# Exchanging the rotary halves by a VectorE shuffle on reordered columns, with the cosines on GpSimd, in a two-layer fp32 transformer block

## The chip, the cores and the metric

The kernel runs on 1 core of one Trainium2 chip. The metric is the device time of one execution in microseconds; the time before is the median of 3 runs. All engine times below are microseconds from the start of the span of one profiled execution.

## The reference

Two layers (`DEPTH = 2`) over 256 tokens `x` and 256 context tokens, model width 1024. Each layer is: a feed-forward block, a mixer, a second feed-forward block, each behind an RMS norm whose shift, scale and gate come from a conditioning vector. The last layer computes no output for the context tokens. The mixer projects the normed tokens by `w_in`; the parts that matter here are the attention's queries and keys:

```python
q = axial_rope(rmsnorm(aq.reshape(B, S, 8, 128), q_norm_w), tabs)
k = axial_rope(rmsnorm(ak.reshape(B, S, 2, 128), k_norm_w), tabs)
kc = rmsnorm(akc.reshape(B, L, 2, 128), k_norm_w)          # context: not rotated

def rotate_pairs(x, cos, sin):            # x: 64 of a head's 128 features
    x1, x2 = jnp.split(x, 2, axis=-1)     # 32 and 32
    return jnp.concatenate([x1 * cos - x2 * sin, x1 * sin + x2 * cos], axis=-1)
```

`axial_rope` does this for the first 64 features with the angle of the token's row and for the last 64 with that of its column. So feature p is combined with feature p + 32 or p - 32. Scores are sums over the 128 features of a head, so any order of the features that q and k share gives the same scores. The rest of the mixer (window attention with a sink, a gated linear attention, two gated branches, an output projection) is not touched.

## The kernel before

One program, written engine by engine, with semaphores set by hand; the order of the work on each engine is the order of the code. Features lie on the 128 partitions and tokens on the free axis (512 in layer 0; in layer 1 the keys and values have 512 and the queries 256).

**Weights.** They stream as 1024 x 256 units, numbered through the program, into `raw` (two buffers by parity). For each unit ScalarE rounds `raw` to `WH` (`prep`, L707, its casts are L718) and VectorE computes the remainder `WL = raw - WH` (`prep`, L1178, its subtractions are L1184). TensorE then forms each product in three passes of matmuls (high x high, high x low, low x high). A unit has two halves e = 0, 1 of 128 columns, which is one output tile (m) each; `hi_ready` and `lo_ready` count the halves, and TensorE waits for the half that it needs. ScalarE's casts and VectorE's subtractions run two units at most ahead.

**The place of the change** is `attn_proj(l)`, the stretch in which the six units `n` to `n + 5` are used: the values (`n`), the keys (`n + 1`) and four units of queries (`n + 2` to `n + 5`, two heads each). The keys are tile pair j = 1, the queries j = 2 to 5. The first two units are used by `first_two`, while the norm's output `hH`, `hL` is still being made: token half c = 0 of unit `n` (L1952 to L1959), then c = 0 of unit `n + 1` (m = 0, then the norm's sums over the partitions for c = 1 at L2121, then m = 1; matmuls L1982, L1983, L1986), then both for c = 1. The norm code of ScalarE and VectorE casts unit `n + 1` between pieces of the norm:

```python
                if n:
                    prep(second, only=0)
                    for kt in range(WAIT_C[n] + 1, KT):
                        square(n, kt, 1)
                    prep(second, only=1)
                    log(1)
```

VectorE has `residual(n, kt, 1)` at the place of `square`, and each square waits for its residual.

Behind that, unit by unit (`unit_cols`, matmuls L1901, L1902, L1907): ScalarE copies a pair's tiles out of PSUM with the norm's weight (`weighted`, L869, into `qrs` for even j and `qn` for odd j), takes squares (`squares`, L851), and rounds the rotated tile (`split`, L883). VectorE normalizes the keys (`k_normed`, L1488), sums squares (`square_sums`, L1504), and computes the remainder (`low`, L1522). The rotation itself takes: `swaps(j)` on TensorE (L2288, two products of a 128 x 128 permutation `swap` with the two tiles, 256 tokens, back into the pair's own PSUM banks), `cosines(j)` (L1499) into `qt[:, e, 0]`, `sines(j)` (L1510) from PSUM into `qt[:, e, 1]` and `rotated(j)` (L1515) on VectorE. Only the 256 `x` tokens are rotated. After the queries come `gate_cols(l, 0, 0)` (L1921 to L1926), its copy out of PSUM on ScalarE (L915, which lets bank 0 go), `scores(l, 0)` (L1887 to L1889), two more gate tiles and the first set of attention, whose transposes are L2323. `q_sums(g)` (L2278) are four small fp32 products that feed ScalarE's `q_rsq(g)`.

## Time and profile before

| | |
|---|---|
| median of 3 runs | 2226.77 us (2226.24 to 2226.85) |
| the profiled execution's own time | 2227.31 us |
| its span in the trace | 2225.5 us |
| TensorE matmuls busy | 2203.2 us (99%) |
| VectorE busy | 1381.4 us (62%) |
| ScalarE busy | 913.7 us (41%) |
| GpSimd busy | 203.7 us (9%) |

Busy shares are means over the whole span. In a row of the timeline the columns are start, duration, engine, line, operation, output <- inputs, shape and count (merged where equal instructions follow each other), and in brackets the engine's idle time just before and what released it. Matmuls are pipelined: the step from one start to the next is what an instruction costs, not the duration printed.

### The profile page before, as it was taken

How to read it: one execution, taken by the hardware profiler on the slowest of the kernel's cores; microseconds unless marked ns; L12 is line 12 of the kernel's file. 1: busy time of each engine (PE TensorE's matmuls, PEld its weight loads, DVE VectorE, ACT ScalarE, POOL GpSimd, SP SyncE). 2: the span in 40 equal slices, each digit the busy share in tenths (PEclk: the TensorE clock that was granted, in tenths of full speed). 3: DMA queues.
4: the chain of work that ended last, by engine and by line, in shares of the span. 5: the costliest groups of instructions: out<-in, count | busy, mean ns of one | idle time of the engine just before them, and what ended most of it. 6: DMA issues, size and time to landing. Idle time of an engine off the chain costs nothing.

```text
span 2225.5 us, 29914 instructions
## 1 busy us (share of the span) xinstructions
PE 2203.2 (99%) x12353; PEld 1920.6 (86%) x12353; DVE 1381.4 (62%) x1863; ACT 913.7 (41%) x1368; POOL 203.7 (9%) x313
## 2 busy tenths in 40 slices
PE   8999999999999999999999999999999999999999
PEld 7888888887888888888888898888889899999997
DVE  6988822667566564586762277655237867666754
ACT  4322212557654454342222153222126766555442
POOL 0000000000332340000000000000000034320000
PEclk9999999999999999999999999999999999999999
DMA  9776533221222222355543336565323233346864
GB/s 325 217 228 195 174 103 100 75 67 41 76 76 76 76 76 76 114 158 183 170 152 103 102 112 195 180 186 165 112 95 94 66 111 114 114 133 181 246 183 159
DMA packets 300385, 300.86 MB, mean 135 GB/s; under 512 B 9648, under 2 KB 267288, under 8 KB 300248
## 3 DMA queue, kind: packets, MB, share of 16 engines
q1 hardware_dynamic: 299648, 298.69, 43.2%
q8 instruction: 98, 1.61, 0.3%
q14 instruction: 39, 0.32, 0.0%
q10 hardware_dynamic: 600, 0.25, 0.0%
HBM read 297.86 MB, written 1.05 MB: 134 GB/s over the span
## 4 chain that ended last, share of the span: by engine, by line
PE 87%; DVE 5%; ACT 3%; DMA 2%; POOL 1%; SPq 1%; issue 1%; ACTq 0%; DVEq 0%
PE PS L1901 13%; PE PS L1907 13%; PE PS L1902 13%; PE PS L1887 6%; PE PS L1889 6%; PE PS L1888 6%; PE PS L1921 4%; PE PS L1926 4%; PE PS L1922 4%; DMA raw<-in_ffn_w 2%; PE PS L2451 2%; DVE WL L1184 1%; PE PS L2510 1%; PE PS L2462 1%; PE PS L2171 1%
## 5 line engine op out<-in xcount | busy, mean ns | idle before, releaser
L1184 DVE TENSOR_TENSOR WL<-raw,WH 128x1024 fp32r<-128x1024 f32 x412 | 499.6, 1249 | 347.7 <-ACT WH L718 347.0
L718 ACT CAST WH<-raw 128x1024 fp32r<-128x1024 f32 x412 | 412.3, 1047 | 383.2 <-PE PS L1889 259.6
L1901 PE MATMUL PS<-hH,WH 128*128 128x512 f32 (+1 forms) x1536 | 541.8, 363 | 0.5 <-DVE sg L1449 0.5
L1902 PE MATMUL PS<-hL,WH 128*128 128x512 f32 (+1 forms) x1536 | 538.3, 361 | 0.0
L1907 PE MATMUL PS<-hH,WL 128*128 128x512 f32 (+1 forms) x1536 | 335.4, 361 | 0.0
L1901 PEld LDWEIGHTS PS<-hH,WH 128*128 128x128 f32 x1536 | 290.0, 189 | 44.7 <-DVE sg L1449 0.9
L1902 PEld LDWEIGHTS PS<-hL,WH 128*128 128x128 f32 x1536 | 290.1, 189 | 43.9 <-issue 0.7
L1907 PEld LDWEIGHTS PS<-hH,WL 128*128 128x128 f32 x1536 | 263.9, 189 | 44.3
L1212 DVE SCALAR_TENSOR_TENSOR mraw<-mraw,cst 128x1024 f32<-128x1024 f32 x196 | 242.3, 1279 | 16.1 <-DMA mraw<-in_w_mod 15.1
L1887 PE MATMUL PS<-hidH,WH 128*128 128x512 f32 (+1 forms) x576 | 214.4, 372 | 0.0
L1888 PE MATMUL PS<-hidL,WH 128*128 128x512 f32 (+1 forms) x576 | 213.9, 371 | 0.0
L1889 PE MATMUL PS<-hidH,WL 128*128 128x512 f32 (+1 forms) x576 | 213.9, 371 | 0.0
L826 ACT ACTIVATE sg<-PS 128x512 f32<-128x512 f32 (+1 forms) x44 | 24.0, 545 | 285.4 <-PE PS L1907 276.8
L1921 PE MATMUL PS<-hH,WH 128*128 128x512 f32 (+1 forms) x384 | 128.2, 347 | 0.0
L1888 PEld LDWEIGHTS PS<-hidL,WH 128*128 128x128 f32 x576 | 108.5, 188 | 19.1
L1887 PEld LDWEIGHTS PS<-hidH,WH 128*128 128x128 f32 x576 | 108.5, 188 | 18.9
L1889 PEld LDWEIGHTS PS<-hidH,WL 128*128 128x128 f32 x576 | 108.5, 188 | 18.5
L1922 PE MATMUL PS<-hL,WH 128*128 128x512 f32 (+1 forms) x384 | 124.3, 336 | 0.0
L820 ACT ACTIVATE sg<-PS 128x512 f32<-128x512 f32 (+1 forms) x44 | 24.0, 545 | 201.5 <-PE PS L1907 197.7
L1453 DVE TENSOR_TENSOR sg<-sg,PS 128x512 f32<-128x512 f32 (+1 forms) x44 | 27.3, 620 | 125.6 <-ACT sg L826 125.4
L1926 PE MATMUL PS<-hH,WL 128*128 128x512 f32 (+1 forms) x384 | 93.0, 336 | 0.0
L1716 DVE TENSOR_TENSOR dq<-dq,gkq 128x1024 f32<-128x1024 f32 (+1 forms) x56 | 61.9, 1107 | 47.1 <-ACT dq L1052 46.6
(277 smaller groups left out, 3504.5 us busy)
## 6 DMA issues: line engine op xcount, KB each, us to landing
raw<-in_ffn_w SPq DMA_DIRECT2D x176, 512.0 KB, 5.3
mraw<-in_w_mod SPq DMA_DIRECT2D x132, 512.0 KB, 4.7
raw<-in_w_in SPq DMA_DIRECT2D x52, 1024.0 KB, 5.2
raw<-in_ffn_w SPq DMA_DIRECT2D x44, 1024.0 KB, 4.9
raw<-in_w_branch_attn SPq DMA_DIRECT2D x8, 1024.0 KB, 5.1
raw<-in_w_branch_gla SPq DMA_DIRECT2D x8, 1024.0 KB, 5.1
raw<-in_w_out SPq DMA_DIRECT2D x8, 1024.0 KB, 5.1
mfirst_b<-in_w_mod SPq DMA_DIRECT2D x8, 512.0 KB, 11.9
```

The costliest lines, as they stand in the source:

```text
L718: nc.scalar.copy(half(WH, n % 2, e, rows), half(raw, n % 2, e, rows)).then_inc(hi_ready, 1)
L1184: nc.vector.tensor_tensor(half(WL, n % 2, e, rows), half(raw, n % 2, e, rows), half(WH, n % 2, e, rows).bitcast(F32), ALU.subtract).then_i ...
L1212: ins = nc.vector.scalar_tensor_tensor(mod_sums(c), mod_buf(p), by, mod_sums(c), ALU.mult, ALU.add)
L1887: mm(o, wh, ah, start=start, stop=False, skip_group_check=rest)
L1888: mm(o, wh, al, start=False, stop=False, skip_group_check=rest)
L1889: return mm(o, wl, ah, start=False, stop=stop, skip_group_check=rest)
L1901: mm(o, wh[:, kt, cols], rh[:, kt, 0:T], start=kt == 0, stop=False)
L1902: mm(o, wh[:, kt, cols], rl[:, kt, 0:T], start=False, stop=False)
L1907: ins = mm(o, wl[:, kt, cols], rh[:, kt, 0:T], start=False, stop=kt == KT - 1)
L1921: mm(o, wh[:, kt, cols], rh[:, kt, 0:T], start=kt == 0, stop=False)
L1922: mm(o, wh[:, kt, cols], rl[:, kt, 0:T], start=False, stop=False)
L1926: ins = mm(o, wl[:, kt, cols], rh[:, kt, 0:T], start=False, stop=kt == KT - 1)
```

## The change

The columns of the keys' and queries' weight units are written in another order when they are cast, so that the two features of a rotation pair lie on neighbouring partitions (feature p and p + 32 at 2b and 2b + 1). The norm weights and the cosine and sine tables are reordered to match. The partner is then fetched within each group of 32 partitions by a `stream_shuffle` on VectorE, from `qn` or `qrs` in SBUF, one instruction for both tiles of a pair. The permutation matrix, its load and `swaps` on TensorE are gone. The product with the cosines is one GpSimd instruction per pair; sine product and sum are one VectorE instruction per pair each.

A reordered unit is no longer cast by column halves: `paired` and `unpaired` take contraction rows (kt 0 to 3, then 4 to 7), so both halves are needed before TensorE can begin either output tile. This holds for the units `n + 1` to `n + 5`. The reads of `raw` step alternately between two columns 32 elements apart.

```diff
+        PAIRED_UNITS = {START[("attn_proj", l)] + j for l in range(DEPTH) for j in range(1, 6)}
+        def paired(t, par, kh):
+            return t[:, par, kh * UN // 2:(kh + 1) * UN // 2].rearrange("p (q b s) -> p q b s", b=P // 4, s=2)
+        def unpaired(par, kh):
+            return raw[:, par, kh * UN // 2:(kh + 1) * UN // 2].rearrange("p (q s b) -> p q b s", s=2, b=P // 4)
...
+            def cosines(l, j):
+                t = tile0 * l + 2 * (j - 1)
+                if j == 1:
+                    pool.wait_ge(qk_n, 2 * (l + 1))
+                else:
+                    pool.wait_ge(q_n, 8 * l + 2 * (j - 1))
+                if t:
+                    pool.wait_ge(qk_rot, t)
+                nc.gpsimd.tensor_tensor(qt[:, :, 0, :], rotated_buf(j)[:, :, 0:S], ropeC[:].unsqueeze(1).to_broadcast([P, 2, S]),
+                                        ALU.mult).then_inc(q_cos, 2)
...
+                    if n in PAIRED_UNITS:
+                        nc.scalar.copy(paired(WH, n % 2, e), unpaired(n % 2, e)).then_inc(hi_ready, 1)
+                        continue
...
+                    if n in PAIRED_UNITS:
+                        nc.vector.tensor_tensor(paired(WL, n % 2, e), unpaired(n % 2, e), paired(WH, n % 2, e).bitcast(F32),
+                                                ALU.subtract).then_inc(lo_ready, 1)
...
+                def shuffled(j):
+                    t = tile0 * l + 2 * (j - 1)
+                    if j == 1:
+                        dve.wait_ge(qk_n, 2 * (l + 1))
+                    else:
+                        dve.wait_ge(q_n, 8 * l + 2 * (j - 1))
+                    if t:
+                        dve.wait_ge(qk_rot, t)
+                    nc.vector.stream_shuffle(qt[:, :, 1, :], rotated_buf(j)[:, :, 0:S], PARTNER).then_inc(qk_shuffled, 2)
+                    dve.wait_ge(qk_shuffled, t + 2)
+                    nc.vector.tensor_tensor(qt[:, :, 1, :], qt[:, :, 1, :], ropeS[:].unsqueeze(1).to_broadcast([P, 2, S]),
+                                            ALU.mult).then_inc(qk_parts, 2)
                 def rotated(j):
-                    for e, (t, T) in enumerate(qk_tiles(l, j)):
-                        dve.wait_ge(qk_parts, t + 1)
-                        nc.vector.tensor_tensor(rotated_buf(j)[:, e, 0:S], qt[:, e, 0, :], qt[:, e, 1, :], ALU.add).then_inc(qk_rot, 1)
+                    t = tile0 * l + 2 * (j - 1)
+                    dve.wait_ge(qk_parts, t + 2)
+                    dve.wait_ge(q_cos, t + 2)
+                    nc.vector.tensor_tensor(rotated_buf(j)[:, :, 0:S], qt[:, :, 0, :], qt[:, :, 1, :], ALU.add).then_inc(qk_rot, 2)
...
                     for m in range(2):
                         cols, o = slice(m * P, (m + 1) * P), PS[:, bank + m * way, own]
-                        pe.wait_ge(hi_ready, 2 * n + 2 + m + 1)
+                        ready = 2 * n + 2 + (1 if n + 1 in PAIRED_UNITS else m) + 1
+                        pe.wait_ge(hi_ready, ready)
...
                 unit_cols(n + 2, 4, hH, hL, qtokens(l))
                 k_sums()
-                unit_cols(n + 3, 0, hH, hL, qtokens(l), between=3 * [nothing] + [lambda: swaps(1)] + 3 * [nothing])
-                swaps(2)
-                pe.wait_ge(qk_parts, tile0 * l + 2)
+                unit_cols(n + 3, 0, hH, hL, qtokens(l))
+                pe.wait_ge(qk_n, 2 * (l + 1))
                 unit_cols(n + 4, 2, hH, hL, qtokens(l))
-                swaps(3)
+                bank_read(2)
+                unit_cols(n + 5, 4, hH, hL, qtokens(l))
                 q_sums(0)
-                pe.wait_ge(qk_parts, tile0 * l + 4)
-                unit_cols(n + 5, 4, hH, hL, qtokens(l))
-                swaps(4)
-                pe.wait_ge(qk_parts, tile0 * l + 6)
+                bank_read(3)
                 gate_cols(l, 0, 0)
-                swaps(5)
+                scores(l, 0)
                 q_sums(1)
-                scores(l, 0)
```

`bank_read(j)` waits for `q_n` and `q_sq` of pair j, that is for `weighted` and `squares`. ScalarE's order of work is the same as before.

On VectorE, here is the stretch of layer 0 from the normalized keys on, before (`qn` and `qrs` are the tiles to be rotated, `qt` the two products, `qred` the sums of squares, `kL` and `actL` remainders):

```order
L1488 SCALAR_TENSOR_TENSOR qn<-PS,vecT,qrs 128x512 x2
L1499 TENSOR_TENSOR qt<-qn,ropeC 128x256 x2
L1504 TENSOR_REDUCE qred<-qsq 128x32
L1510 TENSOR_TENSOR qt<-PS,ropeS 128x256 x2
L1515 TENSOR_TENSOR qn<-qt 128x256 x2
L1184 TENSOR_TENSOR WL<-raw,WH 128x8x128 x2
L1499 TENSOR_TENSOR qt<-qrs,ropeC 128x256 x2
L1522 TENSOR_TENSOR kL<-qn,kH 128x512 x2
L1510 TENSOR_TENSOR qt<-PS,ropeS 128x256 x2
L1515 TENSOR_TENSOR qrs<-qt 128x256 x2
```

And the same stretch of the changed kernel, whose line numbers differ:

```order
L1519 SCALAR_TENSOR_TENSOR qn<-PS,vecT,qrs 128x512 x2
L1536 STREAM_SHUFFLE qt<-qn 128x2x256
L1538 TENSOR_TENSOR qt<-qt,ropeS 128x2x256
L1525 TENSOR_REDUCE qred<-qsq 128x32
L1545 TENSOR_TENSOR qn<-qt 128x2x256
L1212 TENSOR_TENSOR WL<-raw,WH 128x1024 x2
L1536 STREAM_SHUFFLE qt<-qrs 128x2x256
L1538 TENSOR_TENSOR qt<-qt,ropeS 128x2x256
L1552 TENSOR_TENSOR kL<-qn,kH 128x512 x2
L1545 TENSOR_TENSOR qrs<-qt 128x2x256
```

The shuffle has taken the place of the cosines, and the sine product has moved from behind the keys' remainder `kL` to in front of it.

On TensorE, the instructions of layer 0 in which a swap, the small sums or the scores stand, before, each with the semaphores it waits for (the plain matmuls between them left out):

```order
L2288 MATMUL PS<-qn,swap 128x256 [waits q_n,q_sq] x2
L2278 MATMUL PS<-qred,fold 32x16 [waits qk_ln,q_red]
...
L1901 MATMUL PS<-hH,WH 128x512 [waits hi_ready,qk_parts]
...
L2288 MATMUL PS<-qrs,swap 128x256 [waits q_n,q_sq] x2
L1921 MATMUL PS<-hH,WH 128x512 [waits hi_ready,qk_parts]
...
L2278 MATMUL PS<-qred,fold 32x16 [waits qk_ln,q_red]
...
L1887 MATMUL PS<-kH,actH 128x512 [waits ga_raw,qk_parts,qk_ready]
```

In the changed kernel the same stretch reads:

```order
L1929 MATMUL PS<-hH,WH 128x512 [waits hi_ready,q_sq,q_n]
...
L2308 MATMUL PS<-qred,fold 32x16 [waits qk_ln,q_red]
...
L1949 MATMUL PS<-hH,WH 128x512 [waits hi_ready,q_sq,q_n]
...
L1914 MATMUL PS<-kH,actH 128x512 [waits q_sq,ga_raw,q_n,qk_ready]
...
L2308 MATMUL PS<-qred,fold 32x16 [waits qk_ln,q_red]
```

The first small sums now stand behind the last unit of queries and not in front of it, and the second ones behind the scores; no waits on the sine product are left.

## Rows read from the trace of the kernel before

**Rows 1.** The page, part 1: busy time, share of the span, instructions.

```profile
PE 2203.2 (99%) x12353; PEld 1920.6 (86%) x12353; DVE 1381.4 (62%) x1863; ACT 913.7 (41%) x1368; POOL 203.7 (9%) x313
```

**Rows 2.** Timeline of TensorE, layer 1: swaps of j = 1 and j = 2.

```profile
1707.73 1.36 PE L2288 MATMUL PS<-qn,swap 128*128 128x256 f32 x4 [0.41 <-DVE qn L1488]
1708.73 0.47 PE L1901 MATMUL PS<-hH,WH 128*128 128x256 f32 x1
...
1711.79 1.02 PE L2288 MATMUL PS<-qrs,swap 128*128 128x256 f32 x4
1712.46 0.47 PE L1901 MATMUL PS<-hH,WH 128*128 128x256 f32 x1
1712.76 0.28 PE L1902 MATMUL PS<-hL,WH 128*128 128x256 f32 x1
1712.88 0.28 PE L1901 MATMUL PS<-hH,WH 128*128 128x256 f32 x1
```

**Rows 3.** Timeline of TensorE, first product of each tile of unit n + 1, both layers.

```profile
400.74 0.28 PE L1982 MATMUL PS<-hH,WH 128*128 128x256 f32 x1
...
404.78 0.47 PE L1982 MATMUL PS<-hH,WH 128*128 128x256 f32 x1
...
1678.11 0.28 PE L1982 MATMUL PS<-hH,WH 128*128 128x256 f32 x1
```

**Rows 4.** Timeline of ScalarE in the same two stretches.

```profile
399.51 1.03 ACT L718 CAST WH<-raw 128x1024 fp32r<-128x1024 f32 x1
402.45 1.20 ACT L731 ACTIVATE sq<-xT 128x256 f32<-128x256 f32 x3 [1.92 <-DVE xT L1409]
403.56 1.03 ACT L718 CAST WH<-raw 128x1024 fp32r<-128x1024 f32 x1
...
1680.94 1.03 ACT L718 CAST WH<-raw 128x1024 fp32r<-128x1024 f32 x1
```

**Rows 5.** Busy time by engine in a stretch of layer 1 (span, then us busy and instructions).

```profile
1706.90:1732.00 25.10, 24.69 (x192) 22.75 (x191) 25.02 (x51) 17.11 (x36) 0.00 (x0) 1.00 0.42 126
```

**Rows 6.** Timeline of VectorE: beside GpSimd's work in layer 0, and in layer 1.

```profile
400.57 1.46 DVE L1184 TENSOR_TENSOR WL<-raw,WH 128x1024 fp32r<-128x1024 f32 x1 [0.23 <-ACT WH L718]
...
1706.92 1.41 DVE L1488 SCALAR_TENSOR_TENSOR qn<-PS,vecT,qrs 128x512 f32<-128x512 f32 x2 [5.49 <-ACT qrs L860]
...
1708.91 0.70 DVE L1504 TRANSPOSE_TENSOR_REDUCE qred<-qsq 128x16 f32<-128x512 f32 x1
...
1710.84 2.35 DVE L1184 TENSOR_TENSOR WL<-raw,WH 128x1024 fp32r<-128x1024 f32 x2
...
1713.78 1.28 DVE L1522 TENSOR_TENSOR kL<-qn,kH 128x512 fp32r<-128x512 f32 x2
```

**Rows 7.** Timeline of ScalarE, layer 1.

```profile
1708.42 0.84 ACT L869 ACTIVATE qrs<-PS,vecT 128x256 f32<-128x256 f32 x2 [1.02 <-DVE qn L1488]
1709.15 1.99 ACT L718 CAST WH<-raw 128x1024 fp32r<-128x1024 f32 x2
...
1715.16 0.84 ACT L869 ACTIVATE qn<-PS,vecT 128x256 f32<-128x256 f32 x2 [2.98 <-DVE kL L1522]
...
1717.02 2.02 ACT L718 CAST WH<-raw 128x1024 fp32r<-128x1024 f32 x2
```

**Rows 8.** Groups by line and shape, whole span: GpSimd's and VectorE's nearest.

```profile
L640 POOL TENSOR_TENSOR dq<-b 128x512 f32<-128x512 f32 x16 | 19.6, 1243 | 193.1 <-DVE b L1676 193.1
L1584 DVE TENSOR_SCALAR prob<-prob,small 128x512 f32<-128x512 f32 x16 | 7.8, 487 | 0.6
```

**Rows 9.** Timeline of TensorE: first product of the first scores, layers 0 and 1.

```profile
475.42 0.50 PE L1887 MATMUL PS<-kH,actH 128*128 128x512 f32 x1
...
1730.29 0.47 PE L1887 MATMUL PS<-kH,actH 128*128 128x512 f32 x1
```

**Rows 10.** Timeline of ScalarE: the gate tile's copy ahead of those scores.

```profile
474.47 0.59 ACT L915 COPY mraw<-PS 128x512 f32<-128x512 f32 x1 [1.19 <-PE PS L1926]
...
1729.78 0.36 ACT L915 COPY mraw<-PS 128x256 f32<-128x256 f32 x1
```

More of the change, by code:

```diff
@@ L131, in hybrid_backbone @@
         ones = sb("ones", [P, P])
-        swap = sb("swap", [P, P])
+        qred = sb("qred", [P, HEADS * T2 // 32])
         ropeC = sb("ropeC", [P, S])
@@ L548, in _ @@
             sp.dma_start(negsink[:], a["attn_sink"].rearrange("l h -> (l h)").partition_broadcast(P)).then_inc(const_in, 16)
-            for dst, name in ((swap, "c_swap"), (ropeC, "c_cos"), (ropeS, "c_sin"), (amask, "c_amask")):
+            for dst, name in ((ropeC, "c_cos"), (ropeS, "c_sin"), (amask, "c_amask")):
                 sp.dma_start(dst[:], a[name]).then_inc(const_in, 16)
@@ L685, in _ @@
                 add_squares(3 * l + 1)
+                for j in range(1, 6):
+                    cosines(l, j)
                 for i in range(len(SETS[l])):
@@ L1489, in k_normed @@
                                                        ALU.mult, ALU.mult).then_inc(qk_n, 1)
-                def cosines(j):
-                    for e, (t, T) in enumerate(qk_tiles(l, j)):
-                        if j == 1:
-                            dve.wait_ge(qk_n, 2 * l + e + 1)
-                        else:
-                            dve.wait_ge(q_n, 8 * l + 2 * (j - 2) + e + 1)
-                        if t >= 2:
-                            dve.wait_ge(qk_rot, t - 1)
-                        nc.vector.tensor_tensor(qt[:, e, 0, :], rotated_buf(j)[:, e, 0:S], ropeC[:], ALU.mult)
                 def square_sums(j):
@@ L1526, in attn_proj @@
                 k_normed()
-                cosines(1)
+                shuffled(1)
                 square_sums(2)
-                sines(1)
                 rotated(1)
                 prep(n + 4)
-                cosines(2)
+                shuffled(2)
                 low(1)
+                rotated(2)
                 for j in range(3, 6):
@@ L1536, in attn_proj @@
                         prep(n + j + 1)
-                    sines(j - 1)
-                    rotated(j - 1)
-                    cosines(j)
+                    shuffled(j)
                     square_sums(j)
                     low(j - 1)
+                    rotated(j)
                 prep(n + 7, only=0)
-                sines(5)
-                rotated(5)
                 maxima(l, 0)
@@ L1898, in unit_cols @@
                     cols, o = slice(m * P, (m + 1) * P), PS[:, bank + m * step, 0:T]
-                    pe.wait_ge(hi_ready, 2 * n + (m if tiles == 2 else 1) + 1)
+                    ready = 2 * n + (1 if tiles == 1 or n in PAIRED_UNITS else m) + 1
+                    pe.wait_ge(hi_ready, ready)
                     for kt in range(KT):
@@ L1904, in unit_cols @@
                             between.pop(0)()
-                    pe.wait_ge(lo_ready, 2 * n + (m if tiles == 2 else 1) + 1)
+                    pe.wait_ge(lo_ready, ready)
                     for kt in range(KT):
@@ L2279, in q_sums, with bank_read @@
                     ins.then_inc(q_tot, 1)
-                def swaps(j):
-                    for e, (t, T) in enumerate(qk_tiles(l, j)):
-                        if j == 1:
-                            pe.wait_ge(qk_n, 2 * l + e + 1)
-                        else:
-                            pe.wait_ge(q_sq, 8 * l + 2 * (j - 2) + e + 1)
-                            pe.wait_ge(q_n, 8 * l + 2 * (j - 2) + e + 1)
-                        mm(PS[:, 2 * (j % 3) + e, 0:S], swap[:], rotated_buf(j)[:, e, 0:S], start=True, stop=True).then_inc(qk_swap, 1)
+                def bank_read(j):
+                    pe.wait_ge(q_n, 8 * l + 2 * (j - 1))
+                    pe.wait_ge(q_sq, 8 * l + 2 * (j - 1))
                 pe.wait_ge(v_ready, 2 * l + 2)
@@ L2607 @@
            "w_branch_attn", "w_branch_gla", "w_out"]
+PAIRED = np.arange(P).reshape(2, 2, P // 4).transpose(0, 2, 1).reshape(P)
+PARTNER = [i ^ 1 for i in range(32)]
 def shape_constants():
@@ L2619, in shape_constants @@
     sign = np.where(p % half < quarter, -1.0, 1.0).astype(np.float32)[:, None]
-    swap = np.zeros((P, P), np.float32)
-    swap[p, np.where(p % half < quarter, p + quarter, p - quarter)] = 1.0
     q, k = p[:, None], p[None, :]
@@ L2637 @@
     arrays["cond_rows"] = np.concatenate([np.asarray(inputs["c"]).reshape(KT, P), np.asarray(inputs["c_ctx"]).reshape(KT, P)])
+    for name in ("q_norm_w", "k_norm_w"):
+        arrays[name] = np.ascontiguousarray(arrays[name][:, PAIRED])
     arrays.update(shape_constants())
```

27 lines of the change are left out of this document (13 added, 14 removed).

## The prediction, made before the changed kernel had run

> **What bounds the kernel now.** The page's first part comes first: TensorE's matmuls are busy for 2203.2 of 2225.5 us [rows 1]. Time is won only where TensorE gets less to do, and lost wherever it is made to wait. So the question is what the change takes out of TensorE's queue and which waits it puts in. I read TensorE's timeline around the swaps and around the first use of unit n + 1, then the timelines of the engines that feed it there. The second thing to see is that the two layers differ. In layer 0 a query unit takes TensorE about 11 us, and VectorE idles between its pieces. In layer 1 a unit takes half of that, and between 1706.9 and 1732.0 VectorE is busy for 25.02 of 25.10 us, with TensorE at 24.69 [rows 5]. There both engines run level, and nothing done to TensorE alone can shorten the stretch.
>
> **What it removes.** A call of `swaps` costs TensorE 0.67 us from its start to the next product (1711.79 to 1712.46), and the step behind it is 0.30 instead of 0.12, so 0.18 more: 0.85 us [rows 2]. The first call of layer 1 also waits 0.41 for the keys and takes 1.00 to the next product: 0.41 + 1.00 + 0.18 = 1.6 [rows 2]. There are five calls a layer. If TensorE could use all of it, that were 5 x 0.85 = 4.3 in layer 0 and 1.6 + 4 x 0.85 = 5.0 in layer 1, 9.3 together.
>
> Layer 0 keeps most. Its fifth call hides a wait: scores may only start when ScalarE has copied the gate tile out of bank 0, and that copy runs from 474.47 to 475.06 [rows 10], the scores start at 475.42 [rows 9]. Without swaps and small sums ahead of them they can come 0.3 sooner, not 0.85, and the small sums now cost a little by themselves. I take 4 x 0.85 + 0.2 = 3.6 saved.
>
> **The early wait on unit n + 1, both layers.** Before, TensorE starts tile m = 0 of this unit at 400.74, right behind the first cast (399.51 to 400.54), and m = 1 at 404.78, behind the second (403.56 to 404.59) [rows 3, 4]. ScalarE does the second so late because three squares stand ahead of it, which wait for VectorE's residuals (402.45) [rows 4]. The change leaves that order, but m = 0 now needs both casts, since each holds half of the contraction rows. It starts at 404.59 plus 0.1 for the semaphore, 404.7. That is 3.9 later. Behind it stand the norm's sums for c = 1, from which `rstd` and the whole second token half follow, then m = 1. All of these move by the same 3.9, so nothing behind takes it back. Layer 1 has the same picture: the second cast ends at 1681.97, m = 0 started at 1678.11 [rows 3, 4]: 3.9 again. Together +7.8.
>
> **The chain of layer 1.** I keep the old clock and leave out the 3.9. VectorE's list loses `cosines` and gains a shuffle at the same length. The trace has no shuffle of two 256-token tiles; for 512 elements the nearest rows are 0.49 (one input) [rows 8] and half of 1.28, 0.64, for two [rows 6]. It reads and writes one fp32 stream without arithmetic; I take the upper, 0.65 to 0.7, and 1.24 (a GpSimd product of 512 elements [rows 8]) as the far end for an unfamiliar instruction. Sine product and sum are 0.65 each. GpSimd's cosines take 1.24 [rows 8] beside 1.4 to 2 us of VectorE's shuffle, sine product and sum of squares, so `rotated` need not wait. With a shuffle and product of 1.38 in all:
> - Unit n + 4. TensorE could begin at 1711.79 - 1.6 = 1710.2. The casts run 1709.15 to 1711.14 [rows 7], and it needs both: 1711.25, a wait of 1.05. VectorE: keys at 1708.33, shuffle and product to 1709.8, squares 0.63 and sum 0.66 to 1711.0, then 2.35 to 1713.3 [rows 6]. The high products end at 1713.17 (16 x 0.12), another 0.2 for the remainder, then 8 + 24 products of 0.12: the unit ends at 1717.2.
> - Unit n + 5. Its cast stands behind `weighted(3)`, which waits until `low(1)` has read the keys. Before, `low(1)` ended at 1715.06 and `weighted(3)` began at 1715.16 [rows 6, 7]. Now a full shuffle and product (1.38) stands ahead of `low(1)` where cosines of 0.66 stood: 1715.8 and 1715.9. The cast moves with it from 1717.02 to 1717.8 and ends at 1719.8 [rows 7]. TensorE waits 2.6 until 1719.85. VectorE cannot start the third shuffle before 1716.85; 1.38 + squares 0.63 + `low(2)` 0.64 + sum 0.66 bring it to 1720.1, the remainders to 1722.4. TensorE, through with the high products at 1721.8, waits 0.7 more and ends the unit at 1726.3.
> - The scores. `q_sums(0)` now comes behind that unit (0.3), the gate tile takes 24 x 0.12 and ends at 1729.5. ScalarE waits for those sums before `q_rsq(0)` and only then does `weighted(5)`, squares, `split(4)`, a cast of 2.0 and the gate's copy: 1726.8 + 0.5 + 0.8 + 0.65 + 0.65 + 1.9 + 0.36 = 1731.6. Before, the copy started at 1729.78 and the scores at 1730.29 [rows 9, 10]. Now they start at 1731.6: +1.3.
>
> The softmax of the first set hangs on the scores, so the 1.3 stays. Instead of saving 5.0, layer 1 loses 1.3.
>
> **The sum.** +7.8 - 3.6 + 1.3 = +5.5 against the profiled execution's 2227.31, which is 2232.8. The median of the runs is 0.5 below that, so 2232.3. GpSimd's products now run beside VectorE's: a subtraction beside GpSimd's additions took 1.46, while a pair alone takes 2.35, so 1.2 each [rows 6]. Three such meetings of 0.25 lie in layer 1's chain, 0.7 more: **2233.0**. In its own range the shuffle at 0.49 (three on the chain, -0.6) and no slowing give 2231, the shuffle at 1.24 (+1.7) and two more meetings give 2236. SP issues one load less (64 KB), at the start; that costs and gives nothing.
>
> **The rivals.**
> - *The casts themselves are slower.* They read `raw` alternately from two columns 128 bytes apart. No row of the trace reads so on ScalarE or VectorE: every cast here reads runs of 128 columns, so it stays between no cost and twice (cast 1.03 to 2.06, remainder 1.2 to 2.4). Twice: in both layers the first cast ends 1.0 later, its remainder another 1.1, hence residuals and squares, and the second cast 1.0 more: 3.1; its remainder then comes 0.6 after TensorE has run through its high products. That makes 3.9 + 3.7 = 7.6 a layer. In layer 1 the casts of n + 4 and n + 5 add 2.0 each and the remainders about 1, of which 4.8 reach the end of n + 5. Sum: 15.2 - 3.6 + 1.3 + 4.8 = +17.7, **2244.5**. Layer 0's later units have more than 6 us of slack and hide it. The Trainium skill speaks for this rival: "Advanced Engine Details and Errata", Memory Cachelines, says that SBUF is read in lines of 16 bytes, that two hits on a line are needed for full rate and that a new line at each access costs. It gives no size. By it the reads here would pay at every element, and no run so far shows whether they do.
> - *Layer 1's chain is hidden after all* (the one on the other side). If VectorE gets through its list as fast as TensorE shrinks, with the shuffle at the length of a plain one-input row and the casts placed early enough, layer 1 keeps its 5.0: 7.8 - 3.6 - 5.0 = -0.8, **2226**, no change. Its point of decision is `weighted(3)`: it must start by about 1713.3 for TensorE not to wait for unit n + 5, and the 25.02 of 25.10 us speaks against that [rows 5].
> - *The early wait is short.* If the second cast moved up by 3 us, the sum would be about 2227, and with layer 1's chain hidden 2220. ScalarE's order is unchanged and the idle 1.92 ahead of the squares is a wait for VectorE [rows 4], so I see nothing that would move it.
> - *TensorE runs slower after the idle 4 us.* The page shows the full granted clock in all slices, also in those with waits; I give it little.
>
> **How the numbers follow.** The forecast (early wait, layer 1 lost, casts at about their old price) 0.45; casts slower, from a part of the price up to twice, 0.33; layer 1 hidden 0.13; early wait short 0.05; something else, slower still, 0.04. Likeliest is 2233.0, with its own range 2230 to 2236. The range that leaves out 2 in 10 goes from 2227.5 (half of the hidden case falls below) to 2245. A measurement of this kernel can tell about 0.2%, 4.5 us, from no change: 2222.3 and 2231.2 are the limits. Faster: the short wait together with a hidden chain, 0.04. Same: the hidden chain, the short wait alone, and the lower end of the forecast, 0.23. Slower: 0.73.
>
> **What would show it.** In the new profile no swap row; the first product of unit n + 1 about 3.9 us after the last one of unit n, in both layers, with ScalarE's cast as releaser. In layer 1 two new waits of about 1 and 2.6 us on casts ahead of units n + 4 and n + 5, and one of about 2 ahead of the scores; in layer 0 none of these. If casts of 1.03 stay 1.03 in the reordered units, the first rival is dead; if they read 2, it is the case. GpSimd's products should read 1.2 to 2, the shuffle 0.5 to 1.2. The forecast is wrong if TensorE starts unit n + 1 on time, or if layer 1's units follow each other without waits.

## The result, and the profile after

The changed kernel takes 2240.64 us, median of 4 runs (2239.37 to 2241.05), beside 2226.81 for the kernel before on the same chip: ratio 1.006, 95% interval 1.0047 to 1.0074, 13.8 us slower. The forecast was 2233.0: direction and range held, but the loss is more than twice the 6.2 that I had summed. Part 1 of the page:

```profile
PE 2200.5 (98%) x12313; PEld 1917.8 (86%) x12313; DVE 1384.6 (62%) x1843; ACT 917.8 (41%) x1368; POOL 220.8 (10%) x323
```

TensorE has 40 instructions fewer and is busy for 2.7 us less than in [rows 1], and the span is 13.2 longer (2238.7 against 2225.5). So TensorE stands idle for 15.9 us more. The swaps alone had 10.6 us of busy time, so part of what they freed has come back as slower steps. The waits of TensorE by releaser (total, times, longest):

```profile
PE PS L2011 <- ACT WH L740: 8.0, 2, 4.0
...
PE PS L1929 <- ACT WH L740: 4.6, 2, 3.1
...
PE PS L1914 <- ACT mraw L942: 2.5, 2, 1.7
...
PE PS L1935 <- DVE WL L1212: 1.1, 1, 1.1
```

L2011 is the first product of unit n + 1: 4.0 us in each layer, on the cast, as forecast. L1929 and L1935 are the query units, L1914 the scores. The same work on both time axes shows where the loss builds up (starts from the timelines; [rows 3, 9] hold part of before):

| start of | before | after | offset |
|---|---|---|---|
| unit n + 1, layer 0 | 400.74 | 405.07 | +4.3 |
| unit n + 2, layer 0 | 419.45 | 425.31 | +5.9 |
| first scores, layer 0 | 475.42 | 477.44 | +2.0 |
| first transposes, layer 0 | 489.17 | 491.60 | +2.4 |
| unit n + 2, layer 1 | 1696.82 | 1705.82 | +9.0 |
| first scores, layer 1 | 1730.29 | 1744.67 | +14.4 |
| span's end | 2225.5 | 2238.7 | +13.2 |

Layer 1's unit n + 1 starts at 1685.62 for 1678.11 [rows 3], +7.5; less the 4.3 of its own wait the offset ahead of it is 3.2, so 0.8 arises in between, in the gated linear attention, and 1.2 goes again behind layer 1's scores. The change doesn't touch that code; waits there on `mrow` total 2.4 us in this profile and 1.7 in others of similar kernels. I count these pieces, -0.4 in sum, as scatter of one profile.

**Two offsets are not in the forecast.** From unit n + 1 to n + 2 another 1.5 us is lost in layer 0. TensorE's timeline there:

```profile
405.07 0.39 PE L2011 MATMUL PS<-hH,WH 128*128 128x256 f32 x1 [3.98 <-ACT WH L740]
405.30 0.28 PE L2012 MATMUL PS<-hL,WH 128*128 128x256 f32 x1
405.42 0.30 PE L2011 MATMUL PS<-hH,WH 128*128 128x256 f32 x1
...
406.16 0.41 PE L2011 MATMUL PS<-hH,WH 128*128 128x256 f32 x1
406.37 0.41 PE L2012 MATMUL PS<-hL,WH 128*128 128x256 f32 x1
406.58 0.41 PE L2011 MATMUL PS<-hH,WH 128*128 128x256 f32 x1
```

and the windows of both layers (span, busy time and count of PE, PEld, DVE, ACT, POOL, then the granted clock, which is the clock that TensorE gets as a share of 2.4 GHz, DMA share, GB/s):

```profile
405.00:411.00 6.00, 5.93 (x32) 5.77 (x33) 1.24 (x1) 0.02 (x1) 0.00 (x0) 0.72 0.61 180
...
1684.00:1694.00 10.00, 8.38 (x53) 8.23 (x54) 2.55 (x5) 3.37 (x7) 0.96 (x2) 0.83 0.36 111
...
1726.00:1745.00 19.00, 14.25 (x100) 13.50 (x99) 17.24 (x28) 12.59 (x27) 4.35 (x3) 0.82 0.50 159
```

A step of 0.12 becomes 0.21 within 0.7 us of the wait's end: the granted clock has gone from its level of 2.4 GHz to 1.2 GHz, and comes back at about 409.0. The page's row of 40 slices shows nines throughout, and a nine means 90% or more; a slice of 56 us hides 4 slow ones.

The third window shows that the same happens once more, in layer 1's chain. There the clock reads 0.50 from 1729.9 to 1736.7, from inside the wait ahead of unit n + 5 to its second tile:

```profile
1731.11 0.55 PE L1929 MATMUL PS<-hH,WH 128*128 128x256 f32 x1 [3.06 <-ACT WH L740]
1731.46 0.41 PE L1930 MATMUL PS<-hL,WH 128*128 128x256 f32 x1
...
1734.78 2.08 PE L1935 MATMUL PS<-hH,WL 128*128 128x256 f32 x8
```

The slow steps up to 1734.78 cost next to nothing, because the remainders of this unit are ready only then. The eight products behind them take 1.87 us to the next one instead of 0.96, and that 0.9 reaches the scores.

**Layer 1's chain** loses 5.4 us between unit n + 2 and the scores, where I had 2.0. VectorE's timeline:

```profile
1717.45 0.75 DVE L1536 STREAM_SHUFFLE qt<-qn 128x512 f32<-128x512 f32 x1
1718.30 1.00 DVE L1538 TENSOR_TENSOR qt<-qt,ropeS 128x512 f32<-128x512 f32 x1
1719.23 0.70 DVE L1525 TRANSPOSE_TENSOR_REDUCE qred<-qsq 128x16 f32<-128x512 f32 x1
...
1720.43 3.47 DVE L1212 TENSOR_TENSOR WL<-raw,WH 128x1024 fp32r<-128x1024 f32 x2
1723.83 0.01 DVE L1536 LOAD_MASK_SELECT qt<-qrs  x1
...
1724.66 0.69 DVE L1538 TENSOR_TENSOR qt<-qt,ropeS 128x512 f32<-128x512 f32 x1
...
1731.23 3.49 DVE L1212 TENSOR_TENSOR WL<-raw,WH 128x1024 fp32r<-128x1024 f32 x2
```

and GpSimd's:

```profile
1717.46 1.30 POOL L687 TENSOR_TENSOR qt<-qn,ropeC 128x512 f32<-128x512 f32 x1 [32.36 <-issue]
1720.67 2.15 POOL L687 TENSOR_TENSOR qt<-qrs,ropeC 128x512 f32<-128x512 f32 x1 [1.91 <-DVE qn L1545]
1727.62 1.27 POOL L687 TENSOR_TENSOR qt<-qn,ropeC 128x512 f32<-128x512 f32 x1 [4.81 <-ACT qn L896]
1731.83 1.79 POOL L687 TENSOR_TENSOR qt<-qrs,ropeC 128x512 f32<-128x512 f32 x1 [2.94 <-ACT qrs L896]
```

Where before a pair of remainders took 2.35 [rows 6], two pairs take 3.47 and 3.49, the two beside which GpSimd's product stretches to 2.15 and 1.79. A shuffle of 0.75 and a sine product of 1.00 or 0.69 stand for two products of 0.65. By groups (minimum/median/maximum in ns), the reordered casts of ScalarE (L740) beside the plain ones (L745), then the same of VectorE (L1212, L1215):

```profile
L745 ACT CAST WH<-raw x392: 1029/1048/1080, 50.8 to 2224.7; 128x1024 fp32r<-128x1024 f32 x196
L740 ACT CAST WH<-raw x20: 1242/1296/1337, 399.7 to 1729.7; 128x1024 fp32r<-128x1024 f32 x20
...
L1215 DVE TENSOR_TENSOR WL<-raw,WH x392: 1201/1220/2058, 51.8 to 2225.9; 128x1024 fp32r<-128x1024 f32 x196
L1212 DVE TENSOR_TENSOR WL<-raw,WH x20: 1226/1261/2324, 401.0 to 1732.4; 128x1024 fp32r<-128x1024 f32 x20
```

The casts pay a quarter for the reordered read, the remainders 3%; the 2324 is a remainder beside GpSimd's product.

### The profile page after: what moved, and what is told of

Same layout as the page of the kernel before. It is cut to its first block and busy times, and to the rows that moved or that the text cites. A ratio compares the mean times of both kernels' runs of the same rounds, so it can differ in the third digit from the quotient of the medians.

```text
span 2238.7 us, 29833 instructions
## 1 busy us (share of the span) xinstructions
PE 2200.5 (98%) x12313; PEld 1917.8 (86%) x12313; DVE 1384.6 (62%) x1843; ACT 917.8 (41%) x1368; POOL 220.8 (10%) x323
## 3 DMA queue, kind: packets, MB, share of 16 engines
HBM read 297.79 MB, written 1.05 MB: 133 GB/s over the span
## 5 line engine op out<-in xcount | busy, mean ns | idle before, releaser
L1215 DVE TENSOR_TENSOR WL<-raw,WH 128x1024 fp32r<-128x1024 f32 x392 | 473.3, 1245 | 335.2 <-ACT WH L745 334.9
L1929 PE MATMUL PS<-hH,WH 128*128 128x512 f32 (+1 forms) x1536 | 542.4, 363 | 5.3 <-ACT WH L740 4.6
L745 ACT CAST WH<-raw 128x1024 fp32r<-128x1024 f32 x392 | 392.2, 1047 | 370.7 <-PE PS L1916 259.5
L1935 PE MATMUL PS<-hH,WL 128*128 128x512 f32 (+1 forms) x1536 | 336.3, 361 | 1.1 <-DVE WL L1212 1.1
L1929 PEld LDWEIGHTS PS<-hH,WH 128*128 128x128 f32 x1536 | 290.8, 189 | 49.8 <-issue 5.7
L1935 PEld LDWEIGHTS PS<-hH,WL 128*128 128x128 f32 x1536 | 264.5, 189 | 45.7 <-DVE WL L1212 1.5
L1914 PE MATMUL PS<-hidH,WH 128*128 128x512 f32 (+1 forms) x576 | 214.4, 372 | 0.0
L1914 PEld LDWEIGHTS PS<-hidH,WH 128*128 128x128 f32 x576 | 108.5, 188 | 18.7
```

Source lines behind the costliest of these rows:

```text
L745: nc.scalar.copy(half(WH, n % 2, e, rows), half(raw, n % 2, e, rows)).then_inc(hi_ready, 1)
L1215: nc.vector.tensor_tensor(half(WL, n % 2, e, rows), half(raw, n % 2, e, rows), half(WH, n % 2, e, rows).bitcast(F32), ALU.subtract).then_i ...
L1914: mm(o, wh, ah, start=start, stop=False, skip_group_check=rest)
L1929: mm(o, wh[:, kt, cols], rh[:, kt, 0:T], start=kt == 0, stop=False)
L1935: ins = mm(o, wl[:, kt, cols], rh[:, kt, 0:T], start=False, stop=kt == KT - 1)
```

## The experiments

"+x" is the median of a kernel minus that of the kernel before in the same comparison (same chip); for the changed kernel it is +13.8. With intervals of about 0.0012 on the ratio, medians can't resolve less than some 2 us; smaller steps are read from traces. For layer 1 I use one measure throughout: from VectorE's first key product (L1488 before) to its first mask on the scores (L1560 before). It was 25.09 and is 30.48 in the changed kernel. It contains whatever the clock costs in that stretch, so I say where the clock was low.

### The clock: TensorE kept busy through the wait

```diff
                         ready = 2 * n + 2 + (1 if n + 1 in PAIRED_UNITS else m) + 1
+                        if c == 0 and m == 0 and n + 1 in PAIRED_UNITS:
+                            for i in range(31):
+                                mm(o, weights(n % 2)[0][:, i % KT, 0:P], hH[:, i % KT, own], start=True, stop=True)
                         pe.wait_ge(hi_ready, ready)
```

> The changed kernel, with 31 idle products (already cast weights times ready tokens, into the bank that is overwritten anyway) in front of the wait for unit n + 1 in both layers, so that TensorE does not stand still there. Their results are not used. Theory A (the wait of 4.0 us lets the granted clock fall, and the 20 or so products behind it run at half speed): the wait is filled, the clock stays at 1.00, and the time falls by 1.65 us a layer, 3.3 in all, to 2237.4. Theory B (the slower steps after the wait come from something else, weights or tokens read while they are written): the steps stay at 0.21 us and the time stays at 2240.6.

Measured: 2237.84 (+11.0), ratio 1.0049 [1.0034, 1.0064]. The added products' results are overwritten. TensorE now idles 0.34 there. The cast that it waits for ends no sooner, and unit n + 1 starts at 405.27 for 405.07, yet 2.8 us are won back (all four runs, 2237.6 to 2239.1, lie below all four of the changed kernel). Layer 1's low stretch behind the wait of 3.06 is still there. The window of layer 0:

```profile
405.00:411.00 6.00, 5.73 (x43) 5.57 (x44) 1.55 (x2) 1.12 (x3) 0.00 (x0) 1.00 0.59 172
```

### The kernel before with the early wait alone

```diff
-                        pe.wait_ge(hi_ready, 2 * n + 2 + m + 1)
+                        pe.wait_ge(hi_ready, 2 * n + 2 + (1 if norm % 3 == 1 else m) + 1)
-                        pe.wait_ge(lo_ready, 2 * n + 2 + m + 1)
+                        pe.wait_ge(lo_ready, 2 * n + 2 + (1 if norm % 3 == 1 else m) + 1)
```

> The kernel before, with one edit: both tiles of unit n + 1 wait for both halves of the casts. Nothing else of the change is in it. Theory A (wait plus clock): 3.8 + 1.65 a layer, +10.9, 2237.7. Wait alone, with no price of the clock: +7.6, 2234.4. Rival (slack behind takes it back): under +3, below 2230.

Measured: 2237.91 (+11.1), ratio 1.0049 [1.0032, 1.0065]. Waits of 3.74 us, 7.5 in all, cost 11.1: the difference is again the clock (the step after this wait is 0.21; it stays there until about 409.1 in layer 0, 4.7 us, and for 3.4 us in layer 1).

```profile
404.44 0.58 PE L1982 MATMUL PS<-hH,WH 128*128 128x256 f32 x1 [3.74 <-ACT WH L718]
404.82 0.42 PE L1983 MATMUL PS<-hL,WH 128*128 128x256 f32 x1
405.04 0.41 PE L1982 MATMUL PS<-hH,WH 128*128 128x256 f32 x1
```

So the wait itself, with no shuffle, no reordering and no GpSimd product, accounts for four fifths of the loss.

### The changed kernel with unit n + 1 reordered by columns

The permutation stays within the 128 columns of a tile. Unit n + 1 needn't be cast by contraction rows: for it alone, each half e is cast as its own 128 columns, in two instructions by q.

```diff
+                    if n in BY_COLUMNS:
+                        nc.scalar.copy(paired_cols(WH, n % 2, e, 0), unpaired_cols(n % 2, e, 0))
+                        nc.scalar.copy(paired_cols(WH, n % 2, e, 1), unpaired_cols(n % 2, e, 1)).then_inc(hi_ready, 1)
+                        continue
...
-                        ready = 2 * n + 2 + (1 if n + 1 in PAIRED_UNITS else m) + 1
+                        ready = 2 * n + 2 + m + 1
```

> The changed kernel, with unit n + 1 alone cast by column halves again (two instructions of 512 for each half and engine, pairs interleaved as before), so that tile m = 0 needs the first cast only. Theory A (early wait and the clock drop behind it cost 4.0 + 1.65 a layer): a wait of about 0.4 remains, the clock stays up, and the time falls by 5.2 a layer to about 2230.2. Rival (the waits are only moved: the norm's second half or the casts behind it wait instead): at most 2 us are won, 2239.

Measured: 2230.02 (+3.2), ratio 1.0013 [1.0003, 1.0022]. Both early waits are gone, and 10.6 us with them. What is left is layer 0's gain (scores at 472.49, 2.9 sooner than before) against layer 1's chain, which reads 30.74. The low clock behind the wait of 3.06 is in it too, from 1720.0 to 1726.8.

### The kernel before without its swaps

The sine product reads the tile itself instead of its exchanged copy, so the exchange is left out; the order of VectorE's work stays. TensorE's swaps and its waits on them are taken out as well (not shown).

```diff
-                        dve.wait_ge(qk_swap, t + 1)
-                        nc.vector.tensor_tensor(qt[:, e, 1, :], PS[:, 2 * (j % 3) + e, 0:S], ropeS[:], ALU.mult).then_inc(qk_parts, 1)
+                        nc.vector.tensor_tensor(qt[:, e, 1, :], rotated_buf(j)[:, e, 0:S], ropeS[:], ALU.mult).then_inc(qk_parts, 1)
...
```

> The kernel before without the swap products: the sine product reads the unswapped tile from SBUF, so the exchange of the halves is left out of the computation; VectorE's list keeps its length. It shows what taking the swaps from TensorE can bring at most. Theory A (layer 0 keeps nearly all, layer 1 is set by VectorE's list and gets under 1 us): -3.6 to -5, 2222 to 2223.2. Rival (TensorE sets both layers): -9.3, 2217.5.

Measured: 2224.04 (-2.8), ratio 0.9985 [0.9976, 0.9995]. An exchange that costs nothing anywhere wins 2.8 us here, not the 9.3 that TensorE spends on it. Layer 0 gives its 3.7 (scores at 471.73). Layer 1 gives nothing: its measure is 26.12, and TensorE waits where the swaps stood:

```profile
1714.77 0.25 PE L2278 MATMUL PS<-qred,fold 128*32 128x8 f32 x8 [1.45 <-DVE qred L1504]
...
1725.87 0.25 PE L2278 MATMUL PS<-qred,fold 128*32 128x8 f32 x8 [1.76 <-DVE qred L1504]
...
1727.27 0.53 PE L1886 MATMUL PS<-kH,actH 128*128 128x512 f32 x1 [1.15 <-ACT mraw L915]
1727.59 0.63 PE L1887 MATMUL PS<-kL,actH 128*128 128x512 f32 x1
...
1730.04 0.43 DVE L1559 TENSOR_TENSOR PS<-PS,amask 128x256 f32<-128x256 f32 x1 [1.11 <-PE PS L1888]
```

The 1.0 by which the measure is longer than before is the clock's. It is low from 1727.5 to 1730.7, under the scores, and VectorE, through with its list, waits 1.11 for them. At the full clock the measure would be about 25.1, and the ceiling of the idea about 3.8 us, layer 0's saving; that is an estimate from these rows.

### The changed kernel with its cosines on VectorE

```diff
-                for j in range(1, 6):
-                    cosines(l, j)
...
+                    nc.vector.tensor_tensor(qt[:, :, 0, :], rotated_buf(j)[:, :, 0:S], ropeC[:].unsqueeze(1).to_broadcast([P, 2, S]),
+                                            ALU.mult).then_inc(q_cos, 2)
                     nc.vector.stream_shuffle(qt[:, :, 1, :], rotated_buf(j)[:, :, 0:S], PARTNER).then_inc(qk_shuffled, 2)
```

> The changed kernel with its cosine products back on VectorE (one 128x2x256 product ahead of each shuffle) and none on GpSimd. Contention theory: beside GpSimd's products two remainders and one sine product of layer 1's chain lasted 1.1, 1.1 and 0.3 us longer; without them VectorE saves these 2.5 but has three products of 0.65 to 0.7 more ahead of units n + 4 and n + 5, so about 0.4 us less, 2239 to 2240.6. The rival, by which moving the cosines to GpSimd is a plain gain: three products of 0.65 on the chain, 1.9 more, 2242.5.

Measured: 2239.6 (+13.3), ratio 1.0059 [1.0047, 1.0072]. VectorE has five products of 0.62 more in the stretch, and the stretch is 1.4 us shorter, 29.05. Up to the end of unit n + 5's remainders it is 1.0 shorter. Behind that it is 0.4 shorter although two of the five products lie there: in the changed kernel VectorE idles 1.00 ahead of its fifth shuffle, until ScalarE has copied the tiles that TensorE finished late, at the lower level, and here it doesn't. Its timeline, at the place shown above:

```profile
1718.39 0.69 DVE L1538 TENSOR_TENSOR qt<-qt,ropeS 128x512 f32<-128x512 f32 x1
...
1720.20 2.42 DVE L1210 TENSOR_TENSOR WL<-raw,WH 128x1024 fp32r<-128x1024 f32 x2
...
1730.84 2.41 DVE L1210 TENSOR_TENSOR WL<-raw,WH 128x1024 fp32r<-128x1024 f32 x2
```

The remainders are back at 2.4 and the sine product at 0.69. Relief by GpSimd was none here: the five products moved there saved VectorE 3.1, and cost it 3.1 in turn, three times 0.3 on a sine product and twice 1.1 on a pair of remainders.

### The changed kernel with unreordered reads in the casts

```diff
-            return raw[:, par, kh * UN // 2:(kh + 1) * UN // 2].rearrange("p (q s b) -> p q b s", s=2, b=P // 4)
+            return raw[:, par, kh * UN // 2:(kh + 1) * UN // 2].rearrange("p (q b s) -> p q b s", s=2, b=P // 4)
```

The columns then stand in their old order, and the shuffle exchanges the wrong partners; nothing else differs.

> The changed kernel with casts and remainders that read raw in runs of 128 columns (the reordering is left out, the rest is the same). Theory: the casts fall from 1.29 to 1.03 us. In both layers the wait on unit n + 1 falls by two casts, 0.5, to 3.5; in layer 1 two pairs of casts on the chain save 0.5 each: 2.0 in all, 2238.6, if the granted clock still falls after the waits. Rival: the casts' price is hidden in layer 1 and the granted clock decides alone: 2239.6 to 2240.6.

Measured: 2240.14 (+13.9), ratio 1.0061 [1.0048, 1.0074]. The casts read 1.06, the waits on unit n + 1 3.74 and 3.73 (0.25 less each, half of what I had expected), the measure 29.53 (0.95 less), the span 2236.9 (1.8 less). That looks like the theory, but in layer 1 the 0.95 isn't the casts'. TensorE's wait on the casts ahead of unit n + 5 is shorter, 2.63, and one on the remainders has come in its place:

```profile
1729.83 0.35 PE L1929 MATMUL PS<-hH,WH 128*128 128x256 f32 x1 [2.63 <-ACT WH L740]
...
1733.88 1.22 PE L1935 MATMUL PS<-hH,WL 128*128 128x256 f32 x8 [1.90 <-DVE WL L1212]
...
1726.00:1745.00 19.00, 12.79 (x100) 11.73 (x99) 17.89 (x28) 12.79 (x29) 4.37 (x3) 1.00 0.46 143
```

From the keys to the end of these remainders VectorE takes 18.64 us, 18.73 in the changed kernel: the faster casts save 0.1. The other 0.86 lies behind, where the clock is 1.00 here and was low there. And the profiled run isn't typical: it took 2238.82 at a mean clock of 0.998, the other four 2240.0 to 2240.5 at 0.996 to 0.997, so the median doesn't follow. The casts' price is 0.25 in each early wait and 0.1 in layer 1's chain; it isn't the first rival's 11.5.

### low(1) ahead of the second shuffle, on top of the columns

```diff
-                shuffled(2)
                 low(1)
+                shuffled(2)
```

> The kernel with unit n + 1 cast by columns (2230.0) and low(1) ahead of shuffled(2) on VectorE in both layers. Theory: weighted(3) on ScalarE waits for low(1), which now comes 1.4 us sooner; the cast of unit n + 5 moves with it, TensorE's wait ahead of that unit falls from 3.1 to 1.6 us, and the granted clock stays at its upper level behind it: 1.4 to 3 us less, 2227.0 to 2228.6. Rival: the scores of layer 1 hang on VectorE's whole list, in which only the order changes: 2229.5 to 2230.5, with the wait moved to a later place.

Measured: 2230.64 (+4.4), ratio 1.0019 [1.001, 1.0028]. The rival is right and I was wrong: the wait ahead of unit n + 5 fell from 3.06 to 2.54, but one of 1.93 on its remainders came in its place, and the measure is 30.98. The clock didn't fall behind the 2.54, but behind the 1.93 (0.5 from 1726.1 to 1729.5). A piece of VectorE's list moved, its length did not.

### Remainders away from GpSimd's products

Three kernels, each built on the one before it; the first has unit n + 1 cast by columns. Its order of VectorE's work:

```diff
-                prep(n + 4)
                 shuffled(2)
+                prep(n + 4)
                 low(1)
                 rotated(2)
                 for j in range(3, 6):
                     if j > 3:
                         prep(n + j + 1)
+                        rotated(j - 1)
                     shuffled(j)
                     square_sums(j)
                     low(j - 1)
-                    rotated(j)
+                rotated(5)
```

> Unit n + 1 cast by columns (2230.0 as it stands), and VectorE's list in another order: shuffled(2) ahead of the remainders of unit n + 4, rotated(3) and rotated(4) behind the remainders of n + 5 and n + 6. GpSimd's cosine product then falls beside a shuffle and a sine product, and the remainders run with GpSimd idle. Theory (layer 1 was lost to remainders of 3.47 instead of 2.36 us and to what had been put ahead of them): remainders at 2.36, low(1) 1.1 us sooner, TensorE's wait ahead of unit n + 5 2.0 instead of 3.1, no wait or a short one for its remainders, the scores of layer 1 some 3 to 4 us sooner: 2226 to 2227.5. Rival (the shuffles and the longer casts cost as much in any order): 2229 to 2230.5.

> The same with q_sums(0) ahead of unit n + 5 on TensorE, where it waits for a cast anyway, so that ScalarE has rq(0) before the unit ends. Theory: 0.3 us of small products leave the path and 0.5 us of ScalarE's work ahead of weighted(5) in layer 1: 0.5 to 0.8 less than the run before it. Rival: the sums wait for square_sums(3) on VectorE longer than for the cast and push the unit back: 0 to 0.5 more.

> As the run before it, but the reordering casts and remainders go through the elements in the order of raw: they read runs of 32 and write every second element, where they read alternately from two places 128 bytes apart and wrote in sequence. If the 0.25 us a cast comes from the reads, casts read 1.03 to 1.08 us here and the chain of layer 1 saves 0.5 to 1.0; if writing apart costs as much, casts stay at 1.29 or more and the time is the same.

Measured: +2.7 (ratio 1.0011 [1.0002, 1.002]), +2.3 (1.0011 [1.0003, 1.002]) and +1.7 (1.0009 [1.0, 1.0018]). The first was meant to bring layer 1's scores 3 to 4 us sooner and won 0.5 in the time (+3.2 to +2.7), 2.2 in the measure (30.74 to 28.53); remainders read 2.35 to 2.42 in all three and no cosine product on GpSimd is over 1.31. The small sums ahead of the unit aren't told apart from nothing (measure 29.30, with the clock low under the scores). The third read 28.19, at a granted clock of 1.00. Why so little of the measure reaches the time is in the single runs: in four of eleven runs of the first kernel the mean clock is 1.000, and they took 2227.2 to 2228.1; the other seven, at 0.998 to 0.999, took 2229.0 to 2230.6. The second and third kernel split likewise (three runs each at 1.000: 2228.2 to 2228.6, and 2227.0 to 2227.6; the rest up to 2230.8 and 2230.0). So the same kernel keeps the clock in one run and loses it in another, and some 2 us go with it. In its trace the reordering casts and remainders are

```profile
L754 ACT CAST WH<-raw x16: 1104/1150/1188, 415.5 to 1717.8; 128x1024 fp32r<-128x1024 f32 x16
...
L1232 DVE TENSOR_TENSOR WL<-raw,WH x16: 1211/1218/1227, 416.6 to 1720.1; 128x1024 fp32r<-128x1024 f32 x16
```

so reading in runs and writing every second element costs ScalarE 0.1 us a cast instead of 0.25, and VectorE nothing.

### Two more steps on the same way

The first puts `split(4)` on ScalarE behind the gate tile's copy; the second holds GpSimd's second product until `low(1)` is through, goes back to `prep(n + 4)`, `low(1)`, `shuffled(2)`, and places the small sums inside unit n + 5.

```diff
                 prep(n + 7)
                 gate_copy(l, 0, 0)
+                split(4)
                 split(5)
...
+                if j == 2:
+                    pool.wait_ge(qk_ready, tile0 * l + 2)
...
-                q_sums(0)
-                unit_cols(n + 5, 4, hH, hL, qtokens(l))
+                unit_cols(n + 5, 4, hH, hL, qtokens(l), between=3 * [nothing] + [lambda: q_sums(0)] + 3 * [nothing])
```

> As the run before it (2228.4), with split(4) on ScalarE behind the last cast and the gate tile's copy. In layer 1 that copy, for which the scores wait, stood behind split(4), and split(4) behind rotated(4), which I had put behind remainders: ScalarE sat idle 1.22 us there. Theory: the gate copy and the scores of layer 1 come 1.9 us sooner, 2226.5 to 2227.3. Rival: low(4) and the later sets of scores wait for split(4) instead, and the gain is given back: 2228 to 2228.6.

> As the run before it, with low(1) straight behind the remainders of unit n + 4, GpSimd's second cosine product held until low(1) has run, shuffled(2) behind both, and q_sums(0) between the two tiles of unit n + 5. Theory: no remainder meets a GpSimd product, weighted(3) and the cast of unit n + 5 come 1.4 to 2 us sooner, units n + 4 and n + 5 run without a wait for remainders: the stretch from unit n + 2 to the scores of layer 1 falls to 33 to 34.5 us, that of the kernel before (33.5), and layer 0 keeps its 3: 2224 to 2225.5, slightly faster than before. Rival: VectorE's list as a whole is longer by the shuffles and sets the scores all the same: no more than 0.5 below the run before it.

Measured: 2227.63 (+0.9), ratio 1.0005 [0.9996, 1.0013], and 2226.74 (0.0), ratio 1.0002 [0.9993, 1.0011]: the changed scheme made level with the kernel before, not faster. I had hoped for 1 to 2.5 us less. The last one's time is layer 0's saving, 3.2 (scores at 472.23), against layer 1's 3.0 more. On TensorE it takes 34.8 us from unit n + 2 to the scores instead of 38.9; planned were 33 to 34.5, with no wait for remainders, and one of 0.52 is left beside the 2.83 on the cast. The measure stood still from the kernel before these two on, 28.19, 28.21, 28.13, and VectorE runs without a gap from the keys to the mask:

```profile
1704.61 1.41 DVE L1543 SCALAR_TENSOR_TENSOR qn<-PS,vecT,qrs 128x512 f32<-128x512 f32 x2 [5.39 <-ACT qrs L903]
...
1731.60 1.21 DVE L1239 TENSOR_TENSOR WL<-raw,WH 128x1024 fp32r<-128x1024 f32 x1
1732.74 0.42 DVE L1612 TENSOR_TENSOR PS<-PS,amask 128x256 f32<-128x256 f32 x1
```

The scores were ready, their mask came when the list was through. The 3.0 us over 25.09 are the list: in its five rounds, shuffle and sine product take 9.4 us from start to next start where cosine and sine products took 6.7, and the additions of the two products 3.6 for 3.5.

## Why the prediction was right, and where it fell short

| term | forecast | trace |
|---|---|---|
| early wait on unit n + 1, both layers | +7.8 | +11.7 |
| layer 0 without swaps | -3.6 | -3.9, 0.4 given back by the transposes |
| layer 1's chain with GpSimd's meetings | +2.0 | +5.4 |
| scatter | | -0.4 |
| sum | +6.2 | +13.2 |

The measured 2240.64 lies in the outer range, 2227.5 to 2245, but outside the forecast's own, 2230 to 2236. What made the outer range reach so far up was the rival of casts at twice their length, and it wasn't the casts that filled it. The place, the kind and the sign of the loss were foreseen; that the size still fell inside the range is largely luck.

- **The early wait** was right in cause and place: 3.98 and 4.00 us for 3.9, the cast as releaser, in both layers. That it alone makes most of the loss is shown from both sides, by adding it to the kernel before (+11.1) and by removing it from the changed one (-10.6). The step that failed is "TensorE runs slower after the idle 4 us ... I give it little". I took the row of the page with 40 slices as evidence; but behind the first load no wait of the kernel before is longer than 1.5 us, so it couldn't speak for one of 4. It costs 2.8 (the filled wait) to 3.6 us (11.1 less 7.5) in the two early waits, and 0.9 more in layer 1's chain. The rest of the row's excess is the slower casts, 0.25 or so in each layer, and the 0.2 by which the first cast itself came later in layer 0.
- **Layer 0's saving** was right: 3.9 for 3.6, and 3.7 in the kernel without swaps.
- **Layer 1's chain** was right in kind: new waits on casts of 1.56 and 3.06 (forecast 1.05 and 2.6), on remainders 1.06 (forecast 0.9 in two), ahead of the scores 1.7 (about 2). Four terms were too small. "A shuffle and product of 1.38 in all" is 1.44 with GpSimd idle and 1.8 beside it. "Three such meetings of 0.25" were two of 1.1 on remainders, besides 0.3 on each of three sine products. I had the price from a remainder of 1.46 beside GpSimd's additions [rows 6], taking one touch for the typical one. The casts were 0.25 longer each, of which the plain reads show 0.1 to arrive. And the clock, put at nothing, took 0.9.
- **Casts slower by strided reads**, the 0.33 rival, is true to a quarter of its size on ScalarE: 1.29 us, between 1.03 and 2.06, near the lower end; VectorE pays 3%. The Trainium skill, "Advanced Engine Details and Errata", Memory Cachelines, names a penalty without a size. The trace bears out its direction on ScalarE, 1296 against 1048 ns, and hardly on VectorE, 1261 against 1220.
- **Layer 1's chain hidden**, the rival on the other side, is dead, and the evidence was the windows' row: VectorE at 25.02 of 25.10 [rows 5]. Taking work from TensorE there can't pay (measure 26.12 with the swaps gone for nothing, 1.0 of it the clock's), and adding to VectorE costs about one for one (2.9 more in the list, 3.0 in the measure, in the last kernel).
- **Still open**: the 0.4 of scatter, and why the clock falls behind some short waits and not behind others. A version with the changed scheme in layer 0 alone and the old one in layer 1 wasn't tried; from layer 0's 3.7 and layer 1's zero it should lie near the kernel without swaps, 2224, which is an estimate.

## What to carry to other kernels

Ask of each unit of work not only what it costs but by what piece it is handed over: halving by contraction rows instead of by columns cost 11 us for one unit in each layer, at no extra work. Before relieving an engine, look in the window in question for who is full beside it: TensorE's 99% over the span hid that in layer 1 VectorE was the one without a gap, and an exchange moved onto it could only lose there. And TensorE, where it waited for 3 us or more, paid for the wait and then for slower steps behind it; price both. Before a shorter stretch is put down to an edit, compare the granted clock of the two stretches.

## What the runs showed of the hardware

- TensorE's granted clock fell from 2.4 to 1.2 GHz (0.50 in the windows, steps of 0.21 instead of 0.12) at every wait of 3.06 to 4.0 us in these stretches of the two layers. In the changed kernel it was low for 3.4 us behind each early wait, 1.5 us lost each time, and for 6.8 us in and behind the wait of 3.06 in layer 1. Behind shorter waits it went either way: 2.63 (the plain reads) and 2.83 (the last kernel) left it at 1.00, but it fell behind 1.93 (`low(1)` first), 1.95 and 2.41 (remainders away from GpSimd's products) and 1.15 (without swaps). A wait of 2.79 ahead of the scores was followed by it in one kernel and not in the next. The runs draw no clear line, and one kernel does both from run to run (mean clock 1.000 or 0.998).
- GpSimd's product and VectorE's remainders did not share, they took turns: a pair of remainders grew by 1.1, and the GpSimd product by 0.5 to 0.85. Together they last 3.47 and 3.49 us, close to the 2.35 + 1.30 = 3.65 of running one behind the other. A sine product grew with what was left of GpSimd's product at its start: 0.31 longer with 0.46 left, 0.62 longer (1.31) with 0.76 left in the last kernel. Beside the shuffle, which has one input, GpSimd's product stayed at 1.30 and the shuffle at 0.75. The Trainium skill, "SBUF — State Buffer", SBUF: two separate sides, says just this: an operation of VectorE with two inputs in SBUF and one of GpSimd hold a port pair by turns, for the whole instruction. The trace agrees: in each of the two pairs one remainder lasted 2.31 or 2.32 us, the other 1.24 or 1.25. The prediction could have had it from there, and took 0.25 for a meeting instead.
- A shuffle of 128 x 512 fp32 takes 0.72 to 0.77 us, its mask load 0.01, and the next instruction, which depends on it, starts about 0.1 later (1717.45 + 0.75 to 1718.30): more than the 0.49 of a one-input row and than half of the 1.28 [rows 6, 8].
